# Sums of squares in the norms: two channel pieces squared and added in float32 ahead of four broadcast sums on TensorE

## The reference, cut to what matters

```
def rms_norm(x, g):
    y = xf * lax.rsqrt(jnp.mean(xf * xf, axis=-1, keepdims=True) + EPS)
    return (y * g).astype(x.dtype)
h = h + parallel_mixer(rms_norm(h, mix_norm_g), ...)
h = h + memory_cross_attention(rms_norm(h, cross_norm_g), rms_norm(mem, mem_norm_g), ...)
h = h + swiglu_ffn(rms_norm(h, ffn_norm_g), w_gate_up, w_down)
```

## Time and profile before

| | us |
|---|---|
| median of 3 runs | 1018.22 |
| lowest, highest run | 1016.47, 1074.41 |
| profiled execution, its time | 1017.06 |
| span of its slowest core (core 2) | 1015.5 |
| spans of the 8 cores | 1004.2 to 1015.5 |
| PE busy | 957.7 (94%) |
| DVE busy | 425.3 (42%) |
| ACT busy | 385.6 (38%) |
| POOL busy | 170.4 (17%) |

### The profile page before, as it was taken

One profiled execution on the slowest core, in us unless ns is written; L12 is line 12 of the kernel. 1 busy time (PEld: TensorE's weight loads), 2 busy tenths in 40 slices (PEclk: granted clock), 3 DMA queues, 4 the chain that ended last, 5 costly groups with the idle time before them and its releaser, 6 DMA issues.

```text
span 1015.5 us, 16680 instructions; the slowest of 8 cores (1004.2 to 1015.5 us)
## 1 busy us (share of the span) xinstructions
PE 957.7 (94%) x5647; PEld 481.1 (47%) x5752; DVE 425.3 (42%) x934; ACT 385.6 (38%) x726; POOL 170.4 (17%) x253
## 2 busy tenths in 40 slices
PE   2889999999998789999999999999999999999998
PEld 1445545555556675434443444444444444444443
DVE  2436784666764455546677221211133211211111
ACT  3436656555557784446784111111011111111000
POOL 1224452333340011211220000020120000010000
PEclk9989999999998999999999999999999999999999
DMA  9876434110049779300040345547565255538461
GB/s 240 200 126 164 112 53 77 27 38 12 16 107 187 220 211 185 113 0 1 2 84 0 50 76 83 83 76 123 115 115 133 42 83 84 83 60 139 90 133 59
DMA packets 65586, 96.44 MB, mean 95 GB/s; under 512 B 27616, under 2 KB 38752, under 8 KB 63328
## 3 DMA queue, kind: packets, MB, share of 16 engines
q0 software_dynamic: 28496, 50.96, 31.8%
q1 hardware_dynamic: 19968, 40.09, 12.6%
q10 hardware_dynamic: 17040, 4.33, 2.0%
HBM read 133.74 MB, written 12.58 MB: 144 GB/s over the span
## 4 chain that ended last, share of the span: by engine, by line
PE 87%; DMA 4%; issue 2%; ACT 2%; DVE 2%; ACTq 1%; POOL 0%; SPq 0%; DVEq 0%; POOLq 0%
PE psall L306 86%; DMA arena<-v_scr 3%; ACT arena L317 2%; PE psall L309 2%; DMA arena<-xt 1%; DVE arena L335 1%; ACTq L352 1%; DVE arena L324 1%; POOL arena L324 0%; DVE arena L339 0%; DVE arena L329 0%; ACT L317 0%; DVE arena L346 0%; SPq L352 0%; ACTq L203 0%
## 5 line engine op out<-in xcount | busy, mean ns | idle before, releaser
L306 PE MATMUL psall<-arena 128*128 128x512 bf16 (+5 forms) x5327 | 946.0, 335 | 50.9 <-DMA arena<-xt 13.0
L306 PEld LDWEIGHTS psall<-arena 128*128 128x128 bf16 x5432 | 461.0, 100 | 514.4 <-issue 77.6
L317 ACT ACTIVATE arena<-psall 128x512 bf16<-128x512 f32 (+4 forms) x350 | 225.6, 670 | 340.5 <-PE psall L306 316.2
L324 POOL TENSOR_TENSOR arena<-arena 128x256 f32<-128x256 bf16 (+4 forms) x192 | 124.5, 661 | 312.1 <-DVE arena L335 178.0
L324 DVE TENSOR_TENSOR arena<-arena,psall 128x512 bf16<-128x512 f32 x88 | 60.5, 688 | 241.5 <-PE psall L306 232.2
L317 ACT ACTIVATE arena<-arena 128x512 bf16<-128x512 f32 (+6 forms) x292 | 114.2, 410 | 122.2 <-PE psall L306 63.2
L324 DVE TENSOR_TENSOR arena<-psall,arena 128x512 f32<-128x512 f32 (+1 forms) x128 | 86.6, 688 | 172.0 <-PE psall L306 162.5
L335 DVE SCALAR_TENSOR_TENSOR arena<-psall,arena 128x128 bf16<-128x128 f32 (+2 forms) x372 | 111.2, 357 | 61.8 <-ACT arena L317 33.2
L339 DVE TENSOR_REDUCE arena<-arena 128x4 f32<-128x512 bf16 x80 | 54.0, 681 | 50.0 <-ACT arena L317 49.8
L317 ACT ACTIVATE arena<-psall,arena 128x512 bf16<-128x512 f32 (+2 forms) x78 | 52.1, 670 | 39.4 <-PE psall L306 37.3
L355 POOL DMA_DIRECT2D arena<-w_gu_t x22 | 16.6, 753 | 279.1 <-PE psall L306 279.1
(11 more groups left out here) (14 smaller groups left out, 15.8 us busy)
## 6 DMA issues: line engine op xcount, KB each, us to landing
arena<-w_gu_t POOLq DMA_DIRECT2D x22, 1024.0 KB, 8.6
arena<-w_in_t SPq DMA_DIRECT2D x12, 1024.0 KB, 7.6
arena<-w_d_t POOLq DMA_DIRECT2D x8, 1408.0 KB, 17.5
arena<-xr SPq DMA_DIRECT2D x4, 2048.0 KB, 12.3
outT<-arena SPq DMA_DIRECT2D x32, 256.0 KB, 3.6
arena<-xt POOLq DMA_DIRECT2D x7, 1024.0 KB, 12.3
v_scr<-arena ACTq DMA_DIRECT2D x32, 128.0 KB, 2.7
arena<-v_scr SPq DMA_DIRECT2D x4, 1024.0 KB, 8.1
```

The lines of the kernel that those rows point to most:

```text
L306: P.op("pe", lambda e: e.matmul(out, lhsT=lhsT, rhs=rhs, start=start, stop=stop), r, w, max(0.056, 0.003 + size(out) / 2400))
L317: P.op("act", lambda e: e.activation(out=out, in_=in_, func=func, **kw), r, w, 0.18 + 0.00085 * size(out))
L324: P.op(eng, lambda e: e.tensor_tensor(out=out, in0=in0, in1=in1, op=op), r, w, dcost(eng, size(out), per))
```

## The change

In `rms_steps` the channel pieces are taken in pairs, kp = 0 to 3. ACT squares piece 2kp and POOL piece 2kp+1, both into float32 buffers (`rsf`, one for each engine, no second one); DVE adds them and writes the sum in bf16 into one of two buffers `rsq`; one matmul with `ones` adds it over the channels. The steps come in the order square, sum, square, sum, ... and no longer in two blocks of four. A norm has 17 steps in its lane where it had 25. To make room, `rsq` moves to the upper half of its old place, `rsf[1]` lies at Z + 18 KB (earlier `sqb` and `dst`), and the second buffer of the gate's `Silu` output moves from there to 162 KB (earlier `pt`).

```diff
-        rsq = [view(6 * KB + i * KB, 512, BF16) for i in range(4)]
+        rsq = [view(8 * KB + i * KB, 512, BF16) for i in range(2)]
+        rsf = [view(6 * KB, 512, F32), view(Z + 18 * KB, 512, F32)]
...
+        old_rsf = [old_rsq, over([("sqb", i) for i in range(2)] + [("dst", i) for i in range(2)])]
...
+            for kp in range(4):
+                def f(kp=kp):
+                    a, c = rsf[0][:, 0:width], rsf[1][:, 0:width]
+                    ACT(a, src(2 * kp), AF.Square, [srckey(2 * kp)], [("rsf", 0)] + old_rsf[0])
+                    TT("pool", c, src(2 * kp + 1), src(2 * kp + 1), ALU.mult, [srckey(2 * kp + 1)], [("rsf", 1)] + old_rsf[1])
+                    TT("dve", rsq[kp % 2][:, 0:width], a, c, ALU.add, [("rsf", 0), ("rsf", 1)], [("rsq", kp % 2)] + old_rsq)
+                sq.append(f)
+
+                def f2(kp=kp):
+                    MM(psb[bank][:, 0:width], ones, rsq[kp % 2][:, 0:width], kp == 0, kp == 3, [("rsq", kp % 2), "ones"], [("ps", bank)])
+                mm.append(f2)
             for kc in range(8):
-                def f(kc=kc):
-                    o = rsq[kc % 4][:, 0:width]
-                    if kc % 2:
-                        TT("pool", o, src(kc), src(kc), ALU.mult, [srckey(kc)], [("rsq", kc % 4)] + old_rsq)
-                    else:
-                        ACT(o, src(kc), AF.Square, [srckey(kc)], [("rsq", kc % 4)] + old_rsq)
-                sq.append(f)
-
-                def f2(kc=kc):
-                    MM(psb[bank][:, 0:width], ones, rsq[kc % 4][:, 0:width], kc == 0, kc == 7, [("rsq", kc % 4), "ones"], [("ps", bank)])
-                mm.append(f2)
-
                 def h_(kc=kc):
...
-            return sq[0:4] + mm[0:4] + sq[4:8] + mm[4:8] + [g_] + sc
+            return [f for k in range(4) for f in (sq[k], mm[k])] + [g_] + sc
...
-        sgb = [view(Z + 16 * KB + i * 2 * KB, 512, F32) for i in range(2)]
+        sgb = [view(Z + 16 * KB, 512, F32), view(162 * KB, 512, F32)]
...
-                    ACT(sg, psb[gb], AF.Silu, [("ps", gb)], [("sg", n % 2)] + over([("rd", 1)] + [("sqb", i) for i in range(2)] + stage1_small))
+                    ACT(sg, psb[gb], AF.Silu, [("ps", gb)], [("sg", n % 2)] + over([("rd", 1)] + [("pt", i) for i in range(4)] + stage1_small))
```

## The result

The changed kernel took 1014.44 us in the median of 20 runs (1012.32 to 1139.37), the kernel before 1018.01 (1016.14 to 1087.75; 20 runs, the three shown above among them). The forecast was a gain of 5.0 us on the profiled execution, or 6.1 against the median of before. The profiled executions differ by 3.2 us (1017.06 to 1013.88), the medians by 3.6. The time lies in the range and the sign is right, but only about half of the gain came.

What follows compares the result with a forecast made beforehand. PE was taken to bound the kernel. Removed matmuls, 7.34 us, less 1.15 us at the middle stage's end and 1.2 us of short waits, gave 5.0 us off the profiled 1017.06: 1012.1 us, range 1008 to 1018.5.

Steps and rivals of the forecast that it cites:

- What bounds the kernel: Whole kernel: PE bounds it, busy 94% of the span; norm sums cost full matmul time, about 0.2158 us each.
- PE has other work ready nearly everywhere: Reason given for a forecast near the lower bound: little of the 7.34 us removed from PE is lost to waits.
- The clock is no case of its own: Middle stage: the clock stays at its upper level, 1.00, in all stretches, with waits of up to 0.8 us.
- Other losses taken: Middle stage: 1.15 us lost at its end, where DVE is the limit, and 0.2 us at six other sums, 1.2 us.
- Added on DVE, squares: Norms: adds of 0.69 us on DVE, 16.6 us for 24 in the middle stage; POOL's square kept at 1.06 us.
- (a): Rival: the whole saving of 7.34 us comes, since the last norm's adds find gaps of DVE; 1009.7 us, chance 0.22.
- (c): Rival: every middle-stage sum is waited for, 0.57 us late, as adds meet POOL squares; 1023.4 us, chance 0.10.
- (b): Rival: DVE is the limit from 515 us on, so only 1.9 us is gained; 1015.1 us, chance 0.15.
- argument of the single buffer: Norm adds: no square of the same chain runs during an add, since the next square needs the buffer being read.
- (d): Rival: matmuls go but time does not, as the planner leaves gaps in its order; about 1017 us, chance 0.08.

Runs made afterwards that it cites:

- e1: The kernel before, with the residual load of token block 2 booked in the planner as having no bytes; ratio to before 0.9973.
- e2: The changed kernel, with the residual load of token block 2 booked in the planner as having no bytes; ratio to before 0.9928.
- e8: The changed kernel, with the residual load of token block 2 booked at twice its bytes; one run of 1028.6 us.
- e5: The kernel before with four sums a norm over the even pieces only, no adds, and the block 2 load booked at nothing; ratio to before 0.9959.
- e6: e2 with two pairs of float32 buffers, another order of squares and sums, and earlier lanes for two norms; ratio to before 0.9938.
- e10: The changed kernel with all loads booked at 300 instead of 210 GB/s in the planner; median 1002.52 us, ratio to before 0.9835.

## Why the prediction was right or wrong

- **What bounds the kernel: half right.** PE does, and a sum costs nearly full matmul time: 1.60 us for eight (1.73) in the feed-forward part, 4.1 to 4.35 us for the 5.61 of the middle stage once the order lets it (e1 against e2). But what a removed sum brings is set by the order, and this step is missing.
- **"PE has other work ready nearly everywhere": this step failed.** I read PE's 153.4 of 158 us and its 3.6 us of waits as gaps too small to matter, and took 2.35 us of loss in all. The middle stage alone lost 3.64. A small wait can still be the place where the order is pinned. Ahead of the hole stand the sums of the memory norm, `R_steps(0)` and `R_steps(1)`, of which the change removes 0.43 + 8 x 0.2158 = 2.16 us. The loss with the hole is 5.61 - 1.97 = 3.64, without it 5.61 - 4.09 = 1.52; the difference, 2.12, is the saving made ahead of the hole, to 0.04 us, and the hole's waits grew by 2.02. That the hole belongs to the booked landing is shown by taking the landing away (e1, e2) and by moving it (e8). The planner's own total had the short gain in it: its plan ends at 1017.2 us for the kernel before and at 1014.1 for the changed one, 3.1 less; the prediction did not use it.
- **"The clock is no case of its own": wrong.** At 3.8 us of waits close together it falls on six of eight cores, 1.7 us each, and the run is as long as its slowest core. With it the stage gained 0.3 us there. A wait that grows was priced at its own length; here 2.0 us more of waiting brought 1.7 us of half clock with it.
- **Other losses taken: too large, and the place half wrong.** I took 1.15 us at the end of the stage and 1.2 at scattered sums, 2.35 together; without the hole the stage loses 1.5. The waits that PE shows at the end went from 1.03 us (four, before) to 1.25 (five, core 5 after). The rest are the late starts spread over the stage, and they are there without adds (e5, 6.8 us as e2). What makes them was not settled.
- **Added on DVE, squares: right.** 685 ns for an add, 1067 for POOL's square. The price of the adds on the path is at most 0.2 us (e2 against e5). (a), the whole saving, was right for the feed-forward part alone.
- **(c), slower, and (b), DVE the limit: not there.** An add of 685 ns in the mean leaves no room for 0.49 us of contention, and e5 without adds is as long as e2. The rule of the Trainium skill (GPSIMD Engine Reference, Specifications) on shared SBUF interfaces did not reach the adds: on none of the eight cores does one run beside a square of POOL, as the prediction's argument of the single buffer had it. Where the buffers are two (e6), adds do pay, up to 1.53 us, and other `STT` show it in the changed kernel (1.22 us at 442.69 on core 1, with POOL busy from 442.32). (d) was nearest, since it spoke of gaps in the planner's order; it had neither their place nor their cause.

## What to carry to other kernels

Where a planner fixes the order, look for each wait of the bounding engine at what the plan believes there, not only at what the chip does: a landing booked 25 us late swallowed every saving ahead of it here, and no busy share shows it. Compare the booked times of loads with their landings and the DMA share before optimising instructions; here one number (e10 against the changed kernel, 1.4%) was worth five times the change. Ask the planner for its own total before and after the change: where its costs are near the rows, it already holds what the order takes back. A second buffer is no free gain if it lets DVE and POOL meet. When you price a longer gap on PE, add the fall of the clock that it may bring.

## What was not expected of the hardware

- The same waits, 3.8 us within 7, brought the clock down to 1.2 GHz on six cores and left two at 2.4 GHz, in one execution; with 1.8 us of waits (before) on none, with 8.75 us (e8) on all eight, and there twice or for longer on most.
- A bf16 sum of two float32 tiles in SBUF takes the same time on DVE as an add from PSUM (685 and 688 ns), and writing float32 instead of bf16 costs POOL nothing (1067 against 1063 ns) and shows no cost on ACT (630 ns in the mean).
- A DVE add or scaling with both source tensors in SBUF that starts while a 512-element square runs on POOL ends 0.55 us behind that square's end: so in all 32 cases of the kernel before, all 24 of the changed one and all 24 adds of e6 that start so (0.545 to 0.550 us, over the eight cores). One that starts ahead of the square takes its usual time, and so does a scaling whose source is in PSUM (0.75 us).
